# One 512-column product for the low and high token halves in the feed-forward's up units, and the last two up units side by side

## What is computed

```python
D_MODEL, SEQ, DEPTH, D_FF = 1024, 256, 2, 4 * 1024
for l in range(DEPTH):
    ...                                     # convolution, attentions, gates, merge with w_o
    x = layer_norm(DEEPNORM_ALPHA * x + m @ w_o[l], ln1_g[l], ln1_b[l])
    h = jnp.square(jax.nn.relu(x @ w_ff1[l] + b_ff1[l]))
    x = layer_norm(DEEPNORM_ALPHA * x + h @ w_ff2[l] + b_ff2[l], ln2_g[l], ln2_b[l])
return second_block(x, ...)                 # attention over 256 tokens, 32 experts
```

## Time and profile before

| | us |
|---|---|
| median of 3 executions | 1398.06 |
| their range | 1395.46 to 1398.41 |
| the profiled execution, own time | 1402.02 |
| its span, first to last instruction | 1400.2 |
| TensorE busy | 1304.5 |
| VectorE busy | 883.7 |
| ScalarE busy | 586.4 |

### The profile page before, as it was taken

How to read it: one execution, slowest core, us unless ns; L and a number is a source line. 1 busy time by engine, 2 the same in 40 slices (tenths; PEclk the granted TensorE clock), 3 DMA queues, 4 the chain that set the end, 5 groups by cost and what they waited for, 6 DMA issues and landing times.

```text
span 1400.2 us, 22655 instructions
## 1 busy us (share of the span) xinstructions
PE 1304.5 (93%) x9209; PEld 1129.2 (81%) x9209; DVE 883.7 (63%) x1432; ACT 586.4 (42%) x911; POOL 59.7 (4%) x84
## 2 busy tenths in 40 slices
PE   7999999999999799999898999959979989999996
PEld 6999888889999699989888999959878866555553
DVE  3999876865555689996586555565785473232223
ACT  4345673434444434566544444434535343111111
POOL 1000000000000000000000000011033000110100
PEclk9999999999999899999999999989999999999999
DMA  9754434465555356443365555555444666999994
GB/s 289 249 178 142 151 96 146 152 210 183 189 194 183 121 181 205 142 151 106 109 208 180 185 194 191 180 148 167 131 132 142 243 242 255 422 421 420 421 421 199
DMA packets 172584, 289.73 MB, mean 207 GB/s; under 512 B 10388, under 2 KB 143140, under 8 KB 160204
## 3 DMA queue, kind: packets, MB, share of 16 engines
q1 hardware_dynamic: 169580, 281.55, 57.3%
q0 software_dynamic: 2752, 6.82, 1.7%
q10 hardware_dynamic: 160, 0.08, 0.0%
HBM read 287.36 MB, written 3.16 MB: 207 GB/s over the span
## 4 chain that ended last, share of the span: by engine, by line
PE 64%; DVE 23%; ACT 5%; DMA 5%; issue 3%; POOL 0%; SPq 0%; DVEq 0%; ACTq 0%; POOLq 0%
PE ps L1768 16%; PE ps L1769 15%; PE ps L1770 15%; DVE w_lo L1140 7%; PE ps L2240 6%; DVE cvh L1255 5%; ACT w_hi L734 3%; PE ps L2272 3%; DMA w_exp<-in_w_up 2%; DMA raw<-in_w_up 2%; PE ps L2283 2%; DVE nm L1213 1%; DVE gT L1180 1%; PE ps L1783 1%; DVE x_nat L1186 1%
## 5 line engine op out<-in xcount | busy, mean ns | idle before, releaser
L1140 DVE TENSOR_TENSOR w_lo<-raw,w_hi 128x2048 fp32r<-128x2048 f32 (+1 forms) x165 | 369.5, 2239 | 168.6 <-ACT w_hi L734 168.4
L734 ACT ACTIVATE w_hi<-raw 128x2048 fp32r<-128x2048 f32 (+1 forms) x165 | 307.3, 1862 | 246.1 <-PE ps L1770 236.3
L1768 PE MATMUL ps<-xT_hi,w_lo 128*128 128x256 f32 x1176 | 340.0, 289 | 0.0
L1769 PE MATMUL ps<-xT_lo,w_hi 128*128 128x256 f32 x1176 | 333.9, 284 | 0.0
L1770 PE MATMUL ps<-xT_hi,w_hi 128*128 128x256 f32 x1176 | 333.7, 284 | 0.0
L1768 PEld LDWEIGHTS ps<-xT_hi,w_lo 128*128 128x128 f32 x1176 | 226.3, 192 | 8.2 <-issue 7.5
L1769 PEld LDWEIGHTS ps<-xT_lo,w_hi 128*128 128x128 f32 x1176 | 226.6, 193 | 0.4
L1770 PEld LDWEIGHTS ps<-xT_hi,w_hi 128*128 128x128 f32 x1176 | 226.3, 192 | 0.0
L1768 PE MATMUL ps<-w_hi,xT_lo 128*128 128x256 f32 (+2 forms) x536 | 162.1, 302 | 1.9 <-DVE w_lo L1140 1.6
L1769 PE MATMUL ps<-w_lo,xT_hi 128*128 128x256 f32 (+2 forms) x536 | 159.3, 297 | 0.0
L1770 PE MATMUL ps<-w_hi,xT_hi 128*128 128x256 f32 (+2 forms) x536 | 159.2, 297 | 0.0
(11 more groups left out here) (399 smaller groups left out, 1997.5 us busy)
## 6 DMA issues: line engine op xcount, KB each, us to landing
raw<-in_w_in SPq DMA_DIRECT2D x72, 1024.0 KB, 5.2
raw<-in_w_ff SPq DMA_DIRECT2D x64, 1024.0 KB, 5.2
raw<-in_w_down SPq DMA_DIRECT2D x10, 1024.0 KB, 15.3
raw<-in_w_up SPq DMA_DIRECT2D x10, 1024.0 KB, 16.9
w_exp<-in_w_down SPq DMA_DIRECT2D x10, 1024.0 KB, 17.0
raw<-in_w_o SPq DMA_DIRECT2D x8, 1024.0 KB, 4.9
w_exp<-in_w_gate SPq DMA_DIRECT2D x8, 1024.0 KB, 16.2
raw<-in_w_gate SPq DMA_DIRECT2D x8, 1024.0 KB, 17.1
```

Of the source, the lines that this page charges most:

```text
L734: nc.scalar.activation(split_of(u)[0][:, 0:n], raw[:, u % RAW, 0:n], ACT.Copy).then_inc(hi_done, 1)
L1140: nc.vector.tensor_tensor(split_of(u)[1][:, 0:n], raw[:, u % RAW, 0:n], split_of(u)[0][:, 0:n].bitcast(F32), ALU.subtract).then_inc(split_ ...
L1768: nc.tensor.matmul(out_, left[1], right[0], start=start, stop=False)
L1769: nc.tensor.matmul(out_, left[0], right[1], start=False, stop=False)
```

## The change

The two token tiles become one, `xT_both`, in which the low and the high tokens of a chunk lie next to each other (512 columns). A new function `ff1` takes the place of `transposed` for the up units. Per chunk it issues one matmul of 512 moving columns on the high weights (low tokens into columns 0 to 255 of a bank, high tokens into 256 to 511), and one of 256 on the low weights with the high tokens into columns 256 to 511. A half unit has a bank of its own, so an up unit takes banks 4 and 5 or 6 and 7. The two column halves are added at the eviction: ScalarE writes the low half plus bias (Identity in place of ReLU), VectorE adds the high half from PSUM, and a second VectorE instruction does max with 0 and the square. The counter `ff_sq` goes up twice for each up unit. In the first half of the first up unit, where the tokens' high and low parts become ready one after the other, the products stay narrow.

Up 15 moves ahead of down 13: the order is now up 14, up 15, down 13, `last_rows`. The loads follow that order, and the `h_hi` of up 15 waits for down 13, which reads the same buffer.

```diff
--- before.py
+++ after.py
@@ -136,8 +136,8 @@
             w_lo = dense.enter_context(nc.sbuf_tensor("w_lo", [P, SPLIT, UCOLS], F32R))
         w_exp = sb("w_exp", [P, 2 * SPLIT, UCOLS])
 
-        xT_hi = sb("xT_hi", [P, KC, T], F32R)
-        xT_lo = sb("xT_lo", [P, KC, T], F32R)
+        xT_both = sb("xT_both", [P, KC, 2, T], F32R)
+        xT_lo, xT_hi = xT_both[:, :, 0, :], xT_both[:, :, 1, :]
         br_hi = sb("br_hi", [P, 3, CC, T], F32R)
         br_lo = sb("br_lo", [P, 3, CC, T], F32R)
         h_hi = br_hi[:, 0].rearrange("p (s c) t -> p s c t", s=2)
@@ -238,7 +238,7 @@
         seats = wide[:, 3 * D:3 * D + BANK]
         one_hot = br_hi[:, 2].rearrange("p (a c) t -> p a (c t)", a=TT)
         base_i = sb("base_i", [1, N_EXPERTS], I32)
-        y_hi, y_lo = [[x[:, 4 + 2 * h:6 + 2 * h, :].rearrange("p c t -> p (c t)") for h in range(2)] for x in (xT_hi, xT_lo)]
+        y_hi, y_lo = [[xT_both[:, 4 + 2 * h + i].rearrange("p c t -> p (c t)") for h in range(2)] for i in range(2)]
         heT = gT[:, 4, :].rearrange("p (c s) -> p c s", c=2)
         duos = [[qkT[:, 0:2].rearrange("p a c t -> p (a c t)"), qkT[:, 2:4].rearrange("p a c t -> p (a c t)")],
                 [cvh[:, 0:UCOLS], ro[:, 512:512 + UCOLS]],
@@ -550,7 +550,7 @@
                 sp.wait_ge(x_out, l * 8 + 4 + X_CREDIT)
                 for i, name in enumerate(("ln2_g", "ln2_b")):
                     sp.dma_start(lnb[:, i, :], t[name][bass.ds(l, 1), :].rearrange("o d -> (o d)").partition_broadcast(P)).then_inc(lnb2_in, 16)
-                with sp.Fori(0, FFJ // 2 - 1) as i:
+                with sp.Fori(0, FFJ // 2 - 2) as i:
                     for q in range(2):
                         u = U_FF + 3 + 2 * q
                         j = i * 2 + (2 + q)
@@ -558,7 +558,10 @@
                         sp.dma_start(unit3(raw, u % RAW, KC, 256), w_f1[:, bass.ds(l * KC, KC), bass.ds(j * 256, 256)]).then_inc(raw_in[u % RAW], 16)
                         sp.wait_ge(split_done, base + i * 4 + (u + 2))
                         sp.dma_start(unit3(raw, (u + 1) % RAW, 2, D), w_f2[:, bass.ds(l * (D_FF // P) + i * 4 + 2 * (1 + q), 2), :]).then_inc(raw_in[(u + 1) % RAW], 16)
-                ff2(UNITS - 1, FFJ - 1)
+                for q in range(2):
+                    ff1(UNITS - 5 + q, FFJ - 2 + q)
+                for q in range(3):
+                    ff2(UNITS - 3 + q, FFJ - 3 + q)
 
 
             w2 = t["w_in_2"].rearrange("o (k p) n -> p (o k) n", p=P)
@@ -877,11 +880,13 @@
                     act.wait_ge(unit_done, base + i * 4 + (u + 1 + SPLIT_CREDIT))
                     for c in range(2):
                         b = prm[:, C_F1 + 2 * j + c:C_F1 + 2 * j + c + 1] if isinstance(j, int) else prm[:, bass.ds(j * 2 + (C_F1 + c), 1)]
-                        last = nc.scalar.activation(ff_r[:, j0, c * T:(c + 1) * T], ps[:, 4 + j0, c * T:(c + 1) * T], ACT.Relu, bias=b)
+                        last = nc.scalar.activation(ff_r[:, j0, c * T:(c + 1) * T], ps[:, 4 + 2 * j0 + c, 0:T], ACT.Identity, bias=b)
                     last.then_inc(evac_a, 1)
 
                 def square_hi(j, j0):
-                    act.wait_ge(ff_sq, l * FFJ + j + 1)
+                    act.wait_ge(ff_sq, j * 2 + (2 * l * FFJ + 2))
+                    if isinstance(j, int) and j == FFJ - 1:
+                        act.wait_ge(unit_done, base + UNITS - 3 + 1 + SPLIT_CREDIT)
                     nc.scalar.activation(h_hi[:, j0], ff_s[:, j0, :].rearrange("p (c t) -> p c t", c=2), ACT.Copy).then_inc(ff_hi, 1)
 
                 relu(U_FF, 0, 0, 0)
@@ -902,11 +907,10 @@
                             if v == u + 2:
                                 square_hi(j, q)
                 for q in range(2):
-                    u = UNITS - 5 + 2 * q
-                    relu(u, FFJ - 2 + q, 0, q)
-                    split_hi(u + 2)
+                    relu(UNITS - 5 + q, FFJ - 2 + q, 0, q)
+                    split_hi(UNITS - 3 + 2 * q)
                     square_hi(FFJ - 2 + q, q)
-                    split_hi(u + 3)
+                    split_hi(UNITS - 2 + 2 * q)
                 squares(1, 0)
                 split_hi(UNITS + 1)
                 squares(1, 1)
@@ -1322,7 +1326,10 @@
                     if not isinstance(j, int) or j >= 2:
                         dve.wait_ge(ff_lo, l * FFJ + j - 1)
                     dve.wait_ge(evac_a, l * EV_A + EV_A_IN + j + 1)
-                    nc.vector.tensor_tensor(ff_s[:, j0, :], ff_r[:, j0, :], ff_r[:, j0, :], ALU.mult).then_inc(ff_sq, 1)
+                    of_c = [y[:, j0, :].rearrange("p (c t) -> p c t", c=2) for y in (ff_s, ff_r)]
+                    nc.vector.tensor_tensor(of_c[0], of_c[1], ps[:, 4 + 2 * j0:6 + 2 * j0, T:2 * T], ALU.add).then_inc(ff_sq, 1)
+                    dve.wait_ge(ff_sq, j * 2 + (2 * l * FFJ + 1))
+                    nc.vector.scalar_tensor_tensor(out=ff_s[:, j0, :], in0=ff_s[:, j0, :], scalar=0.0, in1=ff_s[:, j0, :], op0=ALU.max, op1=ALU.mult).then_inc(ff_sq, 1)
 
                 def square_lo(j, j0):
                     dve.wait_ge(ff_hi, l * FFJ + j + 1)
@@ -1796,6 +1803,31 @@
                         last = mm3(ps[:, bank, c * T:(c + 1) * T], [x[:, k, cols] for x in w], [x[:, k, :] for x in xT], k == 0, k == KC - 1)
                 last.then_inc(unit_done, 1)
 
+            def ff1(u, j0, ready=None):
+
+                w = weights(u, KC, 256)
+                for c in range(2):
+                    w_c = [x[:, :, c * P:(c + 1) * P] for x in w]
+                    both, high = ps[:, 4 + 2 * j0 + c, :], ps[:, 4 + 2 * j0 + c, T:2 * T]
+                    if ready is not None and c == 0:
+                        for k in range(KC):
+                            if k % 4 == 0:
+                                pe.wait_ge(xT_hid, ready[k // 4])
+                            nc.tensor.matmul(high, w_c[1][:, k, :], xT_hi[:, k, :], start=k == 0, stop=False)
+                            nc.tensor.matmul(high, w_c[0][:, k, :], xT_hi[:, k, :], start=False, stop=k == KC - 1)
+                        for k in range(KC):
+                            if k % 4 == 0:
+                                pe.wait_ge(xT_lod, ready[k // 4])
+                            nc.tensor.matmul(ps[:, 4 + 2 * j0 + c, 0:T], w_c[0][:, k, :], xT_lo[:, k, :], start=k == 0, stop=k == KC - 1)
+                        continue
+                    for k in range(KC):
+                        if k == KC - 1:
+                            nc.tensor.matmul(high, w_c[1][:, k, :], xT_hi[:, k, :], start=False, stop=False)
+                        last = nc.tensor.matmul(both, w_c[0][:, k, :], xT_both[:, k].rearrange("p i t -> p (i t)"), start=k == 0, stop=k == KC - 1)
+                        if k < KC - 1:
+                            nc.tensor.matmul(high, w_c[1][:, k, :], xT_hi[:, k, :], start=False, stop=False)
+                last.then_inc(unit_done, 1)
+
             def natural(u, bank, xT, between=None):
 
                 w = weights(u, KC, 256)
@@ -2002,7 +2034,7 @@
 
                 for j in range(2):
                     ready(U_FF + j)
-                    transposed(U_FF + j, 4 + j, xT, (l * 8 + 7, l * 8 + 8) if j == 0 else None)
+                    ff1(U_FF + j, j, (l * 8 + 7, l * 8 + 8) if j == 0 else None)
                 ff2(0, U_FF + 2, 0, 0, start=True)
                 with pe.Fori(0, FFJ // 2 - 2) as i:
                     for q in range(2):
@@ -2010,15 +2042,15 @@
                         pe.wait_ge(split_done, base + i * 4 + (u + 1 + RAW_CREDIT))
 
                         pe.wait_ge(evac_a, l * EV_A + i * 2 + (EV_A_IN + q + 1))
-                        transposed(u, 4 + q, xT)
+                        ff1(u, q)
                         ff2(1 - q, u + 1, i, i * 2 + (1 + q))
                 for q in range(2):
-                    u = UNITS - 5 + 2 * q
+                    u = UNITS - 5 + q
                     ready(u)
                     pe.wait_ge(evac_a, l * EV_A + EV_A_IN + FFJ - 4 + q + 1)
-                    transposed(u, 4 + q, xT)
-                    if q == 0:
-                        ff2(1, u + 1, 0, FFJ - 3)
+                    pe.wait_ge(ff_sq, 2 * (l * FFJ + FFJ - 4 + q) + 1)
+                    ff1(u, q)
+                ff2(1, UNITS - 3, 0, FFJ - 3)
                 ff2_ready(UNITS - 2, 0, FFJ - 2)
                 last_rows(UNITS - 2, (h_hi[:, 0], h_lo[:, 0]), lambda: ff2_ready(UNITS - 1, 0, FFJ - 1), (h_hi[:, 1], h_lo[:, 1]))
```

## The result

The changed kernel takes 1385.84 us (median of 4 runs, 1385.47 to 1386.06); the kernel before, beside it on the same chip, 1398.24. The ratio is 0.992 [0.9908, 0.9933]. Predicted were 1382.8 and a range of 1379.0 to 1390.0. So the sign, the range and the size are right, but 12.4 us were gained where 15.3 were summed.

What follows compares the result with a forecast made beforehand. TensorE's instruction steps were taken to bound the turns, and VectorE the last part of the stage. Merged products 6.7 us plus the stage's end 8.6 us made 15.3 us, from 1398.06 to 1382.8 us; range 1379 to 1390.

Steps and rivals of the forecast that it cites:

- What bounds the kernel: Feed-forward turns: TensorE's instruction steps, 11.20 of 11.285 us, with the chain eviction, high half, low half taking equal time.
- The merge, 6.7 us: Up units: one wide and one narrow matmul replace three narrow ones, saving 13.5 ns a chunk, 6.7 us for both layers.
- The Trainium skill's 2.5 ns: Overhead of an isolated warm matmul above N/2.4; by it merging the up units' products would save only 1.2 us.
- The eviction: Up units' ScalarE Identity at 470 ns and two VectorE instructions fit a 1.80 us window, 0.2 us spare: cost 0.
- The end, 8.6 us: Last two up units side by side: eviction of up unit 14 to second addition 17.0 us, not 21.5; 8.6 us saved.
- The clock: Stage's end: some 1.7 us of each layer's 4.3 us gain, as a 0.6 us wait leaves the clock up.
- The sum: Whole kernel: 6.7 + 8.6 = 15.3 us saved, median 1398.06 to 1382.8 us; chance 0.70.
- 1: Up units: unequal widths step like three narrow matmuls, so merging saves next to nothing; 1389.5 us, chance 0.08.
- 2: Stage's end: the clock falls even at the shorter wait; 11.9 us saved, 1386.2 us, chance 0.09.
- 3: Up units' eviction: ScalarE's Identity takes 600 ns; 8.5 us saved, 1389.6 us, chance 0.05.
- 5: Up units: narrow matmul waits for the wide one's write to drain, 79 us more, 1462; chance 0.05 together with another.
- 4: Turns: VectorE's longer square pushes the low-half split 0.9 us late, 23 us more, 1406; chance 0.05 together with another.

## Why the prediction came out as it did

- **What bounds the kernel: right.** TensorE's steps set the turn, and the chain eviction, high half, low half stands at zero slack beside it. It already cost 0.05 us in every turn before; taking it away gave 11.28 to 11.22 without the merge and 11.12 to 11.08 with it.
- **The merge, 6.7 us: the mechanism right, the term a third too large.** The step that failed is "Cost on the path: 0.360 before, 0.2265 + 0.1200 = 0.3465 after". A chunk gained 9 ns and not 13.5: 1.95 us per layer in 14 turns and 0.1 in up unit 15, 4.1 us for both layers. The prediction named the weak point (durations from streams of one width) and gave it a rival with the whole term gone, but kept the sum at the rows of each width; the value lay between. The wide matmul by itself was right (0.2265 at the head of an undisturbed up unit). Alternating pairs cost 0.353 in an up unit that starts on time; in the changed kernel about half of the half units did step at the predicted 0.3467, and there the first matmul of a unit lost 0.08 us, against 0.05 before. That growth of the stall is the second part: the prediction saw the chain without slack, but left its cost as it was. With the widths in groups and the chain reordered the term is 12 ns, near the 13.5 summed.
- **The Trainium skill's 2.5 ns: the measurement decides against it here.** By what the Trainium skill, "TensorE: Matmul & The Clock Gate", section "Back-to-back issue gap", gives for an isolated matmul, the merge would have been worth 1.2 us, an estimate. The measured 4.1 lies about midway between that and the 6.7 summed, and would not decide by itself. The 12 ns a chunk with the widths in groups decide: they are near this kernel's rows and far from 2.5.
- **The eviction: right in the turns.** Identity 470 ns, addition 687, square 692, the split 1.80 us behind the addition's start, turn 11.28 with and without the added instruction (both with narrow products). The window had 0.39 us to spare (0.2 said).
- **The end, 8.6 us: right in size.** Predicted was 21.5 to 17.0, of which 0.2 the merge's, measured 21.54 to 17.24: 4.3 less 0.1, 2 x 4.2 = 8.4 us. The wait came out as forecast: 14.08 - 13.50 = 0.58 us of the path were predicted, 0.61 measured (the loader's idle time of 0.84 is not that measure). The starts on its list came 0.1 to 0.2 us late, nearly all of them. The added instruction's 0.7 us per layer at the end was in the prediction's count of VectorE's times, but was not set apart there: the order without the merge leaves no wait at all.
- **The clock: right in its sign, not as firm as told.** The prediction took 1.7 us of each 4.3 for the clock, and tied its fall to the wait of 3.4 us. A wait of 0.84 us never brought it down, but one of 3.4 us sometimes did not either. In the comparison of before and after the 1.7 us were there.
- **The sum.** 4.1 + 8.4 = 12.5 us, as the landmarks give, against 12.4 by the medians.
- **The rivals.** 1 is partly true (9 ns, neither 0 nor 13.5). 2, 3 and 5 didn't happen: clock 1.00, Identity 470 ns, and no drain (the narrow matmul starts 0.234 us behind the wide one, which is listed at 0.40). 4 needed the 1.21 us that one experiment added.

## What to carry to other kernels

Take the step of an instruction from the place where it will run: streams of one width made an alternating pair up to 6 ns too cheap, on a term of 13.5 ns; where widths must mix, put them in groups. Before you call a step the price of an instruction, compare it over all units of the trace: here one kernel had two values for the same pair. An instruction added to an engine that is half idle is free in a turn whose chain has a gap for it and full price where that engine works without a break, so cost it at each place apart. Where a chain has no slack, look whether work that nobody waits for yet stands ahead of work that TensorE needs next; moving it behind took the stall away in both kernels.

## What the runs showed of the hardware

- Two executions with the same wait of TensorE (3.03 and 3.04 us) and the same busy times in it, one with the clock granted at 1.00 behind it, one at 0.50; 19.81 against 22.28 us for the end of the stage. So a gain that rests on the clock can come or go with an edit that leaves the wait's length alone.
- A wide matmul and the narrow one behind it cost 0.353 us alternating, in up units whose first matmul comes on time, and 0.3475 in groups of eight; the sum of their own streams is 0.3465. In the changed kernel 27 of 52 half units alternated at 0.3467 all the same. A group of wide ones behind narrow ones costs 0.02 to 0.03 us once.
- A VectorE instruction that waits for the one ahead of it on VectorE started 0.72 us behind that one's start (386.52 to 387.24). Without such a wait two 128x512 instructions start 0.605 us apart (380.79 to 382.00 for two), although each is listed at 0.69. So the wait costs 0.11 us of VectorE's time, inside the 0.1 to 0.2 that the prediction estimated; beside the listed duration it looks like 0.03.
